# Attention weights turned over by products with a diagonal of reciprocals, in place of a scaling on VectorE and transposes

## The chip, the cores and the metric

The kernel runs on one core of one Trainium2 chip. The metric is the device time of one execution in microseconds. A core has TensorE for matrix products (the profile shows it as PE, and its weight loads as PEld), VectorE (DVE), ScalarE (ACT), GpSimd (POOL), and SyncE (SP), which issues the large transfers.

## The reference, cut to what matters

Two networks run one after the other on 256 tokens of width 1024. The change lies in the first of them (`first_block`, depth 2), and there only in its attention:

```
def attention(q, k, v, scale):
    ...
    def one_block(qi):
        s = jnp.einsum('bhgqd,bhkd->bhgqk', qi, k, preferred_element_type=jnp.float32) * scale
        p = jax.nn.softmax(s, axis=-1)
        return jnp.einsum('bhgqk,bhkd->bhgqd', p.astype(v.dtype), v)
```

There are 12 heads: 6 with a head width of 64 that share 2 key heads, and 6 with query and key width 96 and a value width of 64. In layer 0 both the 256 context tokens (which see 256 keys) and the 256 latent tokens (which see all 512 keys) go through attention. In layer 1 only the latent tokens do. Everything is computed in float32.

## The kernel before

One program with a list of instructions for each engine, written out by hand. The engines are tied together by semaphores alone, and each engine works through its list in order. The weights of the model stream through a ring of three 2 MB slots; ScalarE and VectorE split each granule of them into two parts, and most products on TensorE are three passes over such parts (lines 1367 to 1369).

The attention of layer `i` (lines 1548 to 1608 for TensorE) is a loop over steps `j`. A step has one pair of heads, one set of tokens and 128 queries, and so two units `u = 2j` and `2j+1`, one for each head. A unit has 128 queries in the partitions and its keys, 256 or 512, along the row. Layer 0 has 24 steps (12 with 256 keys, 12 with 512) and 48 units; layer 1 has 12 steps with 512 keys and 24 units. In its step `j` each engine does this:

- TensorE: the score products of units 2j and 2j+1 into banks 0 to 3 (line 1574; 64 rows for the first three pairs of heads, whose two products lie side by side in the array, 96 rows for the other three); in layer 0 now and then a part of a modulation row (lines 1326 and 1336); then, for units 2j-4 and 2j-3, once `p_ready` says that the unit's weights are ready, one 128x128 transpose for each 128 keys into bank 4 or 5 (line 1592); and every second step the product of the values with the transposed weights of the group before (line 1606, 256 columns).
- VectorE: the negated maximum of each row of units 2j and 2j+1 (line 2760); then, for units 2j-2 and 2j-1, the reciprocal of the row sum (line 2770) and the scaling of the whole row of weights by it (line 2771), which raises `p_ready`; then copies of finished outputs, modulation rows, and shares of the split of the coming weights.
- ScalarE: the copy of the transposed weights of units 2j-4 and 2j-3 out of their banks (line 2106); then the exponential of units 2j and 2j+1 with its row sum (line 2116).

The weights of a unit lie in one of four buffers (`weights(u)`: three in `pb`, one in `sq`). ScalarE writes unit `u` only after the transposes of unit `u-4` are done. `turns2` is a tile of 128x512 numbers that this stage does not use otherwise; its flat view `t2_flat` serves the stage before.

In all the two layers transpose 24 x 2 + 24 x 4 + 24 x 4 = 240 blocks of 128x128.

Of the kernel before, what the change touches and what calls it, by code (L numbers as in the profile page):

```python
# [11 lines left out]
ALU = mybir.AluOpType  # L12
# [3 lines left out]
P = 128  # L16
# [410 lines left out]
def program(nc, A, out):  # L427
# [5 lines left out]
    with ExitStack() as ctx:  # L433
# [53 lines left out]
        IDENT = cc("ident")  # L487
# [44 lines left out]
        t2_flat = turns2[:, :, :, :].rearrange("p a b c -> p (a b c)")  # L532
# [22 lines left out]
        qm_ss, qm_ms, qm_r, qm_r2, qm_c = (stat_of(o, MH) for o in (232, 256, 280, 304, 328))  # L555
        q_ms, q_r, q_r2 = (stat_of(o, GQ) for o in (352, 376, 400))
        sq_flat = sq[:, :, :].rearrange("p a t -> p (a t)")

        def squared_at(n, w):
            return sq_flat[:, 768 * (n % 2):768 * (n % 2) + w]  # L560
# [157 lines left out]
        p_ready = sem("p_ready")  # L718
# [43 lines left out]
        def weights(u):  # L762

            return pb[:, u % 4, :] if u % 4 < 3 else sq[:, 2, :]
# [57 lines left out]
        for _, _, product in granules:  # L822
            if product:
                b, n = use[product]
# [34 lines left out]
        for key in slots:  # L859
# [6 lines left out]
            else:  # L866
                b, n = use[last_product(key)]
# [383 lines left out]
        def _(pe):  # L1251
# [149 lines left out]
            for i in range(DEPTH):  # L1401
# [154 lines left out]
                for j in range(steps + 3):  # L1556
                    if j < steps:
                        pair, s = groups[j // 2]
                        if pair[0] == GQ and s == 0 and j % 2 == 0:

                            for h in range(MH):
                                await_drained(pe, (tag, "Tkm", h))
                                await_drained(pe, (tag, "Tqm", h))
                            for t in range(4):
                                await_drained(pe, (tag, "kvv", t))
                        q0, tiles = sets[s][0] + j % 2 * P, sets[s][1]
                        banks = [start_bank((tag, "s", 2 * j + e)) for e in range(2)]
                        for e, h in enumerate(pair):
                            if h < GQ:
                                rows = slice(HD * (h // 3), HD * (h // 3) + HD)  # L1570
                                lhs, rhs = qT[rows, h % 3, q0:q0 + P], kT[rows, 0:tiles * P]
                            else:
                                lhs, rhs = qmT[0:MQK, h - GQ, q0:q0 + P], kmT[0:MQK, h - GQ, 0:tiles * P]
                            fill(mm(banks[e][:, 0:tiles * P], lhs, rhs, start=True, stop=True), (tag, "s", 2 * j + e))  # L1574


                    if i == 0:
                        if j < 2:
                            mod_column(MOD_FIRST + j)
                        if j in MOD_STEPS:  # L1580
                            mod_products(MOD_STEPS[j], range(0, 4))
                        if j - 1 in MOD_STEPS:
                            mod_products(MOD_STEPS[j - 1], range(4, KC))
                        if j - 3 in MOD_STEPS:
                            mod_column(MOD_STEPS[j - 3])
                    if 0 <= j - 2 < steps:
                        tiles = sets[groups[(j - 2) // 2][1]][1]
                        for u in (2 * j - 4, 2 * j - 3):
                            b = start_bank((tag, "t", u))
                            pe.wait_ge(p_ready, p_base + u + 1)  # L1590
                            for t in range(tiles):
                                last = tr(b[:, t * P:(t + 1) * P], weights(u)[:, t * P:(t + 1) * P], IDENT)
                            fill(last, (tag, "t", u))
                    g, odd = divmod(j - 4, 2)
                    if 0 <= g < len(groups) and not odd:
                        pair, s = groups[g]
                        tiles = sets[s][1]
                        b = start_bank((tag, "o", g))
                        for u in range(4 * g, 4 * g + 4):
                            await_drained(pe, (tag, "t", u))  # L1600
                        for t in range(tiles):
                            for e, h in enumerate(pair):
                                rows = slice(64 * (h % 2), 64 * (h % 2) + 64)
                                v = v_tok[:, t, HD * (h // 3):HD * (h // 3) + HD] if h < GQ else \
                                    vm_tok[:, t, MV * (h - GQ):MV * (h - GQ) + MV]
                                last = mm(b[rows, 0:SEQ], v, weights_T(g, e)[:, t, :], start=(t == 0), stop=(t == tiles - 1))  # L1606
                        fill(last, (tag, "o", g))
                    c = j - steps
                    if 0 <= c < 2:
                        key = (tag, "pool", c)  # L1610
                        b = start_bank(key)
                        if c == 0:
                            pooled_seen[0] += 2 * (2 - s0)
                            pe.wait_ge(pooled, pooled_seen[0])
                        for s in range(s0, 2):
                            last = mm(b[:, s * SEQ:(s + 1) * SEQ], w_pool[:, i, c, :], upad[:, c, s, PAD:PAD + SEQ],
                                      start=True, stop=True)
                        fill(last, key)
# [756 lines left out]
        def _(dve):  # L2375
# [353 lines left out]
            for i in range(DEPTH):  # L2729
# [24 lines left out]
                for j in range(steps + 3):  # L2754
                    if j < steps:
                        keys = sets[groups[j // 2][1]][1] * P
                        for u in (2 * j, 2 * j + 1):
                            st = stat[:, 8 * (u % 8):8 * (u % 8) + 8]
                            await_bank(dve, (tag, "s", u))
                            V.tensor_reduce(st[:, 2:3], bank((tag, "s", u))[:, 0:keys], AX_X, ALU.max, negate=True)\  # L2760
                                .then_inc(nmax_ready, 1)
                    if i == 0 and j == 1:
                        for n in MOD_UNITS:
                            mod_biased(0, 4 * n, 4 * n + 4, ("modcol", n))
                    if 1 <= j <= steps:
                        keys = sets[groups[(j - 1) // 2][1]][1] * P
                        for u in (2 * j - 2, 2 * j - 1):
                            st = stat[:, 8 * (u % 8):8 * (u % 8) + 8]
                            await_drained(dve, (tag, "s", u))
                            link(V.reciprocal(st[:, 6:7], st[:, 4:5]))  # L2770
                            V.tensor_scalar(weights(u)[:, 0:keys], weights(u)[:, 0:keys], st[:, 6:7], None, ALU.mult)\
                                .then_inc(p_ready, 1)
                    if i == 0 and j - 1 in MOD_STEPS:
                        mod_row_copied(MOD_STEPS[j - 1])
                    if i == 0 and j - 3 in MOD_STEPS:
                        n = MOD_STEPS[j - 3]
                        mod_biased(0, 4 * n, 4 * n + 4, ("modcol", n))
                    c = j - steps - 1
                    if 0 <= c < 2:
                        key = (tag, "pool", c)  # L2780
                        await_bank(dve, key)
                        cols = slice(s0 * SEQ, TOK)
                        drain(V.tensor_scalar(mixT[:, 6 + c, cols], bank(key)[:, cols], gain(i, RA["ls"] + c), None,
                                              ALU.mult), key)
                    g, odd = divmod(j - 4, 2)
                    if 0 <= g < len(groups) and not odd:
                        pair, s = groups[g]
                        q0 = sets[s][0]
                        key = (tag, "o", g)
                        await_bank(dve, key)  # L2790
                        if pair[0] < GQ:
                            for h in pair:
                                rows = slice(64 * (h % 2), 64 * (h % 2) + 64)
                                last = V.tensor_copy(mixT[rows, h // 2, q0:q0 + SEQ], bank(key)[rows, 0:SEQ])
                        else:
                            last = V.tensor_copy(mixT[:, pair[0] // 2, q0:q0 + SEQ], bank(key)[:, 0:SEQ])
                        drain(last, key)
                    if j - 1 in MIX_STEPS[i]:
                        mix_rest()
                    if j == steps - 2:  # L2800
                        lo_to(first_gran["wout", i] + 1)
                    if j == steps + 1:
                        lo_to(first_gran["wout", i] + 2)
# [298 lines left out]
```

## Time and profile before

| | |
|---|---|
| time, median of 3 runs | 1700.58 us (1699.9 to 1702.26) |
| the profiled execution | 1699.19 us, with a span of 1697.4 us |
| PE busy | 1635.2 us (96%) |
| VectorE busy | 1149.6 us (68%) |
| ScalarE busy | 905.7 us (53%) |
| the two attention stages | about 129.4 to 211.1 us and 699.5 to 741.3 us |

Busy time of PE counts an instruction from its start to its modelled end, and ends overlap the next starts; so two back-to-back products take less from start to start than the duration that a row shows. A float32 product leaves two records of MATMUL in the trace, and a float32 transpose one.

### The profile page before, as it was taken

Reading aid. Unit: us, or ns where it says so; the run is one execution under the profiler, and the core shown is the slowest. Engines: PE = TensorE matmul, PEld = TensorE weight load, DVE = VectorE, ACT = ScalarE, POOL = GpSimd, SP = SyncE. Lnnn points to the kernel's source line nnn. Section 1 sums busy time; section 2 is a strip of 40 time slices with the busy share of each in tenths; the row PEclk is TensorE's granted clock in tenths of the full one; section 3 lists DMA queues with packets and bytes.
Section 4 is the critical chain, followed back from the end, with each engine's and each line's share of the span. In section 5 each row is a group of like instructions: output and inputs, shape, how many; then the busy total and the mean of one; then the engine's idle time right before and its main releaser. Section 6 shows DMA issues by size and latency. Waiting matters only on the chain.

```text
span 1697.4 us, 27974 instructions
## 1 busy us (share of the span) xinstructions
PE 1635.2 (96%) x10354; PEld 1403.1 (83%) x10354; DVE 1149.6 (68%) x2027; ACT 905.7 (53%) x1970; POOL 487.4 (29%) x936
## 2 busy tenths in 40 slices
PE   6998998999999999898999999999999999999998
PEld 3874586888888878577999887998899878999998
DVE  5668848877787347866555678785556787775555
ACT  4456725444353535756555666675444665764542
POOL 1432013000000022402000134277753161586720
PEclk9999999999999999999999999999999999999999
DMA  9524224555445222114545445442255445343450
GB/s 363 181 88 161 100 98 154 198 199 198 176 176 183 101 87 100 50 58 144 197 164 186 166 146 199 150 145 105 101 199 193 163 155 176 123 142 108 150 199 26
DMA packets 106393, 254.95 MB, mean 150 GB/s; under 512 B 2758, under 2 KB 9556, under 8 KB 103188
## 3 DMA queue, kind: packets, MB, share of 16 engines
q1 hardware_dynamic: 104890, 250.57, 41.4%
q0 software_dynamic: 1088, 2.56, 0.7%
q8 instruction: 84, 1.38, 0.3%
q14 instruction: 49, 0.40, 0.1%
q10 hardware_dynamic: 282, 0.04, 0.0%
HBM read 252.11 MB, written 1.05 MB: 149 GB/s over the span
## 4 chain that ended last, share of the span: by engine, by line
PE 51%; DVE 7%; ACT 3%; issue 1%; POOL 1%; DVEq 0%; ACTq 0%; POOLq 0%
PE ps L1367 12%; PE ps L1369 11%; PE ps L1368 11%; PE ps L1670 2%; PE ps L1671 2%; PE ps L1672 2%; DVE big_r L2522 2%; PE ps L1789 1%; PE ps L1792 1%; PE ps L1784 1%; ACT big_r L1901 1%; PE ps L1574 1%; DVE cst_r L2522 1%; DVE hT_r L2522 1%; PE ps L1606 1%
## 5 line engine op out<-in xcount | busy, mean ns | idle before, releaser
L1901 ACT ACTIVATE big_r<-ring 128x1024 fp32r<-128x1024 f32 (+2 forms) x224 | 234.9, 1049 | 373.1 <-PE ps L1369 352.9
L2522 DVE TENSOR_TENSOR big_r<-ring,big_r 128x1024 fp32r<-128x1024 f32 (+2 forms) x224 | 275.3, 1229 | 226.3 <-ACT big_r L1901 225.8
L1368 PE MATMUL ps<-big_r 128*128 128x256 f32 (+1 forms) x1064 | 352.9, 332 | 0.0
L1367 PE MATMUL ps<-hT_r,big_r 128*128 128x256 f32 (+1 forms) x768 | 245.7, 320 | 0.4 <-DVE big_r L2522 0.4
L1367 PE MATMUL ps<-big_r 128*128 128x256 f32 (+1 forms) x720 | 240.4, 334 | 3.6 <-DVE big_r L2522 1.7
L1369 PE MATMUL ps<-hT_r,big_r 128*128 128x256 f32 (+1 forms) x768 | 242.1, 315 | 0.0
L1369 PE MATMUL ps<-big_r 128*128 128x256 f32 (+1 forms) x720 | 237.9, 330 | 0.0
L1030 POOL TENSOR_TENSOR sq<-sq 128x256 f32<-128x256 f32 (+1 forms) x30 | 35.5, 1185 | 696.7 <-ACT sq L1858 695.1
L1368 PEld LDWEIGHTS ps<-big_r 128*128 128x128 f32 x1064 | 202.2, 190 | 18.3
L1367 PEld LDWEIGHTS ps<-hT_r,big_r 128*128 128x128 f32 x768 | 146.3, 190 | 9.6 <-issue 1.0
L1369 PEld LDWEIGHTS ps<-hT_r,big_r 128*128 128x128 f32 x768 | 146.2, 190 | 9.3
L1367 PEld LDWEIGHTS ps<-big_r 128*128 128x128 f32 x720 | 136.7, 190 | 18.5 <-issue 3.3
L1369 PEld LDWEIGHTS ps<-big_r 128*128 128x128 f32 x720 | 136.8, 190 | 12.8
L2522 DVE TENSOR_TENSOR cst_r<-ring,w_ukv_sb_r 128x1024 fp32r<-128x1024 f32 x70 | 88.5, 1265 | 54.1 <-ACT w_ukv_sb_r L1901 54.1
L1901 ACT ACTIVATE w_ukv_sb_r<-ring 128x1024 fp32r<-128x1024 f32 x70 | 74.0, 1057 | 85.5 <-PE ps L1369 73.4
L2488 DVE SCALAR_TENSOR_TENSOR pT<-ring,csilu,pT 128x512 f32<-128x512 f32 x168 | 118.4, 746 | 1.3
L1901 ACT ACTIVATE nt_r<-ring 128x1024 fp32r<-128x1024 f32 (+2 forms) x54 | 55.8, 1034 | 77.7 <-PE ps L1369 73.2
L2522 DVE TENSOR_TENSOR rstd_r<-ring,nt_r 128x1024 fp32r<-128x1024 f32 (+2 forms) x54 | 65.5, 1212 | 45.4 <-ACT nt_r L1901 45.3
L1367 PE MATMUL ps<-hT_r,w_ukv_sb_r 128*128 128x256 f32 x304 | 88.3, 290 | 0.0
L1369 PE MATMUL ps<-hT_r,cst_r 128*128 128x256 f32 x304 | 85.9, 283 | 0.0
L1368 PE MATMUL ps<-xT_r,nt_r 128*128 128x256 f32 x304 | 85.6, 282 | 0.0
L1368 PE MATMUL ps<-xT_r,w_ukv_sb_r 128*128 128x256 f32 x296 | 83.6, 283 | 0.0
(432 smaller groups left out, 4264.2 us busy)
## 6 DMA issues: line engine op xcount, KB each, us to landing
ring<-in_w_in SPq DMA_DIRECT2D x42, 2048.0 KB, 7.9
ring<-in_w_mlp SPq DMA_DIRECT2D x32, 2048.0 KB, 8.7
ring<-in_w_mod SPq DMA_DIRECT2D x24, 2048.0 KB, 7.9
ring<-in_w_out SPq DMA_DIRECT2D x4, 2048.0 KB, 7.9
ring<-in_w_out_a SPq DMA_DIRECT2D x4, 2048.0 KB, 7.9
ring<-in_w_out_b SPq DMA_DIRECT2D x4, 2048.0 KB, 8.1
ring<-in_w_o SPq DMA_DIRECT2D x4, 2048.0 KB, 8.1
ring<-in_w_in SPq DMA_DIRECT2D x2, 1536.0 KB, 14.2
```

Source lines behind the costliest of these rows:

```text
L1030: nc.gpsimd.tensor_tensor(sum_slot(0, T), sum_slot(0, T), sum_slot(k, T), ALU.add).then_inc(sq_summed, 1)
L1367: mm(b[:, 0:T], w_hi[:, k, :], hi(k), start=(j == 0), stop=False)
L1368: mm(b[:, 0:T], w_hi[:, k, :], lo(k), start=False, stop=False)
L1369: last = mm(b[:, 0:T], w_lo[:, k, :], hi(k), start=False, stop=(j == KC - 1))
L1574: fill(mm(banks[e][:, 0:tiles * P], lhs, rhs, start=True, stop=True), (tag, "s", 2 * j + e))
L1606: last = mm(b[rows, 0:SEQ], v, weights_T(g, e)[:, t, :], start=(t == 0), stop=(t == tiles - 1))
L1670: mm(o, x0, y_hi, start=(m == 0 and k == 0), stop=False)
L1671: mm(o, x0, y_lo, start=False, stop=False)
L1672: last = mm(o, x1, y_hi, start=False, stop=(m == 3 and k == 1))
L1901: act_fn(hi, raw, ACT.Copy).then_inc(hi_ready, 1)
L2488: ins = V.scalar_tensor_tensor(acc, w, c, acc, ALU.mult, ALU.add)
L2522: V.tensor_tensor(lo, raw, hi.bitcast(F32), ALU.subtract).then_inc(lo_ready, 1)
```

## The change

The row of weights is no longer scaled. VectorE instead scales the 128x128 identity by the reciprocals, which gives a matrix with the reciprocals on its diagonal (`normaliser(u)`, one of four in `turns2`), and raises `p_ready` after that. TensorE then computes the product of the transposed block of weights with this matrix, which is the transposed block with each query's column scaled. It writes the same bank, in the same place of the order. Nothing else in the order of any engine changes, and no wait is added or taken away.

```
+        def normaliser(u):
+
+            return t2_flat[:, P * (u % 4):P * (u % 4) + P]
...
                             b = start_bank((tag, "t", u))
                             pe.wait_ge(p_ready, p_base + u + 1)
                             for t in range(tiles):
-                                last = tr(b[:, t * P:(t + 1) * P], weights(u)[:, t * P:(t + 1) * P], IDENT)
+                                last = mm(b[:, t * P:(t + 1) * P], weights(u)[:, t * P:(t + 1) * P], normaliser(u),
+                                          start=True, stop=True)
                             fill(last, (tag, "t", u))
...
                             st = stat[:, 8 * (u % 8):8 * (u % 8) + 8]
                             await_drained(dve, (tag, "s", u))
                             link(V.reciprocal(st[:, 6:7], st[:, 4:5]))
-                            V.tensor_scalar(weights(u)[:, 0:keys], weights(u)[:, 0:keys], st[:, 6:7], None, ALU.mult)\
-                                .then_inc(p_ready, 1)
+                            V.tensor_scalar(normaliser(u), IDENT, st[:, 6:7], None, ALU.mult).then_inc(p_ready, 1)
```

## Rows read from the trace of the kernel before

**Rows 1.** The page, busy time: us, share of the span, instructions.

```profile
PE 1635.2 (96%) x10354; PEld 1403.1 (83%) x10354; DVE 1149.6 (68%) x2027; ACT 905.7 (53%) x1970; POOL 487.4 (29%) x936
```

**Rows 2.** Windows over both attention stages: length, busy us of each engine, clock.

```profile
core 0: us, PE busy (x) PEld busy (x) DVE busy (x) ACT busy (x) POOL busy (x), PEclk, DMA share, GB/s
129.40:143.00 13.60, 10.51 (x64) 4.75 (x64) 12.00 (x28) 6.73 (x21) 10.15 (x12) 1.00 0.72 281
143.00:203.00 60.00, 59.25 (x370) 32.45 (x368) 50.69 (x147) 40.75 (x120) 0.00 (x0) 1.00 0.30 106
203.00:211.10 8.10, 6.95 (x49) 4.89 (x49) 6.19 (x14) 6.41 (x14) 0.00 (x0) 1.00 0.01 2
699.50:706.80 7.30, 6.69 (x35) 3.39 (x36) 7.09 (x18) 6.30 (x17) 5.35 (x8) 1.00 0.00 0
706.80:732.80 26.00, 26.00 (x151) 15.04 (x149) 21.58 (x53) 18.55 (x46) 0.00 (x0) 1.00 0.01 2
732.80:741.30 8.50, 6.96 (x54) 4.69 (x53) 5.95 (x16) 6.76 (x16) 0.00 (x0) 1.00 0.01 3
```

**Rows 3.** The transposes' line, L1592: ns min/median/max, and who waits for them.

```profile
L1592 PEld LDWEIGHTS ps<-cst,pb x180: 137/140/144, 135.7 to 737.7; 128*128 128x128 f32 x180
L1592 PE MATMUL ps<-cst,pb x180: 270/273/331, 135.8 to 737.8; 128*128 128x128 f32 x180
...
L1592 PE MATMUL ps<-cst,sq x60: 271/273/300, 139.6 to 738.2; 128*128 128x128 f32 x60
...
  DVE pb L2771: 5.6, 7
```

**Rows 4.** Timeline of PE, second network: three float32 products of 128x128 blocks.

```profile
1107.59 0.39 PE L1765 MATMUL ps<-big,pT 128*128 128x128 f32 x2
1107.81 0.39 PE L1766 MATMUL ps<-big,pT 128*128 128x128 f32 x2
1108.04 0.39 PE L1767 MATMUL ps<-big,pT 128*128 128x128 f32 x2
```

**Rows 5.** L1765's weight loads: ns min/median/max.

```profile
L1765 PEld LDWEIGHTS ps<-big,pT x64: 188/191/192, 1087.8 to 1603.8; 128*128 128x128 f32 x64
```

**Rows 6.** Timeline of PE, end of layer 1's attention; idle before in brackets.

```profile
731.79 0.60 PE L1592 MATMUL ps<-cst,pb 128*128 128x128 f32 x4
732.23 0.60 PE L1592 MATMUL ps<-cst,sq 128*128 128x128 f32 x4
733.91 1.22 PE L1592 MATMUL ps<-cst,pb 128*128 128x128 f32 x8 [1.08 <-DVE pb L2771]
...
739.41 0.40 PE L1606 MATMUL ps<-rstd,big 128*64 128x256 f32 x1 [0.46 <-ACT nt L2106]
```

**Rows 7.** Timeline of PE, start of layer 0's attention.

```profile
135.77 0.41 PE L1592 MATMUL ps<-cst,pb 128*128 128x128 f32 x2 [0.76 <-DVE pb L2771]
136.56 0.41 PE L1592 MATMUL ps<-cst,pb 128*128 128x128 f32 x2 [0.39 <-DVE pb L2771]
...
141.97 1.22 PE L1592 MATMUL ps<-cst,pb 128*128 128x128 f32 x8 [0.76 <-DVE pb L2771]
```

**Rows 8.** Timeline of PE, the two other waits of layer 0.

```profile
164.63 1.22 PE L1592 MATMUL ps<-cst,pb 128*128 128x128 f32 x8 [0.60 <-DVE pb L2771]
...
204.13 1.22 PE L1592 MATMUL ps<-cst,pb 128*128 128x128 f32 x8 [1.25 <-DVE pb L2771]
```

**Rows 9.** Timeline of PE, layer 1: eight transposes at its start, and eight later.

```profile
700.64 1.40 PE L1592 MATMUL ps<-cst,pb 128*128 128x128 f32 x8
...
712.60 1.04 PE L1592 MATMUL ps<-cst,pb 128*128 128x128 f32 x8
```

**Rows 10.** Timeline of DVE: the scaling beside a busy POOL, and alone.

```profile
134.38 1.25 DVE L2771 TENSOR_SCALAR pb<-pb,stat 128x256 f32<-128x256 f32 x1
...
137.72 0.91 DVE L2771 TENSOR_SCALAR pb<-pb,stat 128x256 f32<-128x256 f32 x1
...
195.74 0.35 DVE L2771 TENSOR_SCALAR pb<-pb,stat 128x256 f32<-128x256 f32 x1
...
203.50 0.49 DVE L2771 TENSOR_SCALAR pb<-pb,stat 128x512 f32<-128x512 f32 x1
```

**Rows 11.** Waits in 129 to 212 us: total us, times, longest.

```profile
ACT pT L2106 <- PE ps L1592: 17.9, 11, 3.3
```

## The prediction, made before the run

> **What bounds the kernel now.** I read the busy shares first: PE is busy for 96% of the span and VectorE for 68% [rows 1], so the kernel as a whole is TensorE's. That share is an average, and the change touches two stages only, so I then cut the two attention stages into windows [rows 2]. Each has three parts. In the long middle parts (143 to 203 us and 706.8 to 732.8 us) PE is busy for 59.25 of 60.00 us and 26.00 of 26.00 us at a granted clock of 1.00, while VectorE has 50.69 and 21.58 us of work: TensorE sets the pace. At the starts it is the other way round: from 129.4 to 143 us PE has 10.51 of 13.6 us and VectorE 12.00, and from 699.5 to 706.8 us VectorE is at 7.09 of 7.30. At the ends neither is full. Next the question of who waits for whom at the changed lines. The transposes waited for the scaling 5.6 us in 7 waits [rows 3], and nearly all of that stands at the places shown in [rows 6 to 8]; ScalarE, which copies the transposed blocks out, waited for the transposes 17.9 us in layer 0 alone [rows 11]. So a slower turning-over is paid by TensorE directly through most of both stages, and a quicker preparation on VectorE pays only at the starts and in three other waits.
>
> **What one block costs before.** A row gives a transpose 273 ns [rows 3], but these overlap. Two groups of four start at 731.79 and 732.23 us [rows 6]: 0.44 us for four, 0.11 us for a block. Likewise eight take 1.04 us, and (1.04 - 0.27) / 7 is 0.11 [rows 9].
>
> **What one block costs after.** The trace has the very form elsewhere: a float32 product with 128x128 stationary weights and 128 moving columns [rows 4]. Each leaves two records, and the three start at 1107.59, 1107.81 and 1108.04 us: 0.45 us for two, 0.225 us for one; the rounding of the rows allows 0.22 to 0.23. I take 0.2225, twice the 0.11 us between its records (0.39 us for two less the 0.275 of one gives 0.11 to 0.12). So a block costs 0.1125 us more. 240 blocks [rows 3] make 27.0 us if TensorE is the bound at every one.
>
> A rule speaks to this. The Trainium skill, TensorE: Matmul & The Clock Gate, in Terms, says that the transpose mode is four times as fast for FP32 as the ordinary one. By that rule, with 0.2225 us for the product, a transpose would take 0.056 us and the change would cost 0.167 x 240 = 40 us. The row has 0.11 us for the transpose, so the row's factor of two goes into the sum.
>
> **Part by part.** Where TensorE waits for VectorE, the longer products fill the wait. I go through the stretches of [rows 2].
>
> - Middle parts: layer 0 has 16 of its 144 blocks before and 16 behind, layer 1 24 and 16 of its 96. That leaves 112 and 56: 168 x 0.1125 = +18.9 us. One wait of 0.60 us lies inside, at 164.63 us [rows 8]; the four products before it take 0.45 us longer and the diagonal is ready 0.2 us earlier (below), so it goes: -0.6. Together +18.3.
> - Start of layer 0: 16 blocks, +1.8 us of PE. But PE waits here five times for the scaling, 0.76, 0.39, 0.75, 0.39 and 0.76 us, the first two and the last in [rows 7]. VectorE sets the pace, beside a busy GpSimd (10.15 of 13.6 us). The second product of each pair starts after a wait, so most of the 1.8 us is hidden, and only some 0.9 us of it, at 142 us, comes after the last wait. VectorE itself gets quicker: four scalings of 256 columns that take up to 1.25 and 0.91 us here against 0.35 us alone [rows 10] become 128 columns wide. I take 0.35 to 0.4 us off each, 1.5 in all. Net -0.6 us.
> - Start of layer 1: 24 blocks, +2.7 us. Eight transposes take 1.40 us there against 1.04 later [rows 9], so 0.36 us in these eight is waiting, and the two steps behind them wait about as much; 1.2 us of waiting vanishes because TensorE becomes the slower. Net +1.5 us.
> - End of layer 0: 16 blocks, +1.8 us. The wait of 1.25 us at 204.13 [rows 8] shrinks by the 0.45 us of the four blocks before it and the 0.2 us of the quicker VectorE, and a short wait between the two units goes (0.13): net +1.0.
> - End of layer 1: 16 blocks, +1.8 us. The wait of 1.08 us at 733.91 [rows 6] has eight blocks before it, 0.9 us, and with 0.2 us from VectorE it is gone; the wait of 0.46 us for ScalarE's copy at 739.41 shrinks by some 0.3, and 0.1 goes between units. Net +0.3 to +0.4.
> - Restarts: a product's weight load takes 191 ns [rows 5], a transpose's 140 [rows 3]. In the row of products the load hides; at the head of a group, behind another shape, it shows. 36 steps x 0.05 us is 1.8 us; I keep +1.0, since the rest falls into waits.
>
> The sum is 18.3 - 0.6 + 1.5 + 1.0 + 0.3 + 1.0 = **+21.5 us**.
>
> **VectorE's own saving** is larger than what the path sees. A row of 512 takes 0.49 us and one of 256 0.35 us [rows 10], so 0.14 us for 256 columns; 128 columns would take 0.28. 48 units save 0.21 us and 24 save 0.07: 11.8 us. In the middle parts it is worth nothing, because VectorE already idles there (50.69 of 60 us). The identity is read in place of the weights, so ScalarE's buffers come free no later than before, except that TensorE holds them 0.45 us longer for a unit, and ScalarE, with 40.75 of 60 us, has room for that. No DMA is issued or moved.
>
> The profiled execution was 1699.19 us, 1.4 us under the median. From the median, 1700.6 + 21.5 = **1722.1**.
>
> **The rivals.**
> 1. *VectorE is the real bound.* Its lists hold the reductions, copies and splits that TensorE needs, and it is at 84% in the middle of layer 0. Then the doubled products hide, the 11.8 us come off, and the time is 1689. It speaks against this that PE's busy time leaves 0.75 us in 60, and that ScalarE waits 17.9 us for transposes. It decides only if PE has more than 0.45 us of hidden slack in a step of two key tiles and 0.9 us in one of four. 4%.
> 2. *The second record hides.* If a product cost what a transpose costs in this place, only the waits would change: 6.6 us of them at most, and about 2 us by what VectorE gives back; 1697 to 1701. The three rows in a line [rows 4] speak against it. 3%.
> 3. *More is absorbed.* Waits that the modelled ends hide (PE's 59.25 us of busy time count overlap) take up another 5 to 11 us: 1710 to 1716. 10%.
> 4. *The weight loads bind.* If a load must end before the next begins, a block costs 2 x 0.19 = 0.38 us, +0.27 a block and +65 us at most: 1765. In [rows 4] the records start every 0.11 us with those very loads, so 3%; the partial case, restarts dearer than I count and nothing absorbed (27.0 + 3.6), ends at 1731. Both together 6%.
> 5. *A transpose is quicker than its spacing.* If 0.11 us were set by the 140 ns of its weight load and half of it were slack of the array, the product would cost three blocks' time more, not one: 0.167 x 240 = 40 us, 1740. In the trace eight transposes and the products around them follow each other at 0.11 us whether they stand in fours or in eights [rows 6, 9], so I see no such slack: 2%. It is what the Trainium skill's factor of four (TensorE: Matmul & The Clock Gate, Terms) would give.
>
> **How the numbers follow.** The forecast, slower by 15 to 29 us, has 75%. Its low end has every wait at the changed lines absorbed (27.0 less 6.6 us of waits and 3.5 of waits hidden in modelled ends: 1717.5), its high end almost nothing absorbed and all restarts paid (27.0 + 1.8: 1729.4). The range 1715.5 to 1729.5 takes in the near edge of rival 3 and leaves out the rest of the rivals and the tails of the forecast, 2 in 10. A measurement of this kernel tells 0.2%, 3.4 us, from no change. Slower by more than that: 93%; within: 3%; faster: 4%.
>
> **What would show it.** In the profile after, the changed line should have 480 records in place of 240, 0.11 us apart, with weight loads of 190 ns. Attention of layer 0 should last about 12.5 us longer and that of layer 1 about 8.5; the stretches outside should keep their lengths. VectorE's busy time should fall by some 11 us with no gain from it, a diagonal should take 0.28 us, and the waits at 164, 204 and 734 us should shrink or go. Starts of units still 0.11 us a block, or attention stages that keep their lengths, would prove the sum wrong; a stage that grows by more than 27 us in total would show the loads or a wait that I do not see.

## The result, and the profile after

| | before | after |
|---|---|---|
| time, median | 1700.99 us (4 runs) | 1721.24 us (4 runs, 1720.43 to 1725.96) |
| ratio to before | | 1.0127, 95% interval 1.0113 to 1.0140 |
| the profiled execution: time | 1699.19 us | 1720.43 us |
| its span | 1697.4 us | 1718.6 us |

The kernel is slower by 20 to 22 us: the medians differ by 20.3 and the ratio makes 21.6. The forecast was 21.5.

The page of the kernel after, busy time (it answers to [rows 1]):

```profile
PE 1660.2 (97%) x10594; PEld 1432.9 (83%) x10594; DVE 1140.5 (66%) x2027; ACT 908.2 (53%) x1970; POOL 485.2 (28%) x936
```

PE has 240 records more and 25 us more of busy time; VectorE has 9.1 us less, and the kernel is no quicker for it.

Windows of the kernel after, cut where the stretches of [rows 2] ended (before and behind the middle of each stage):

```profile
core 0: us, PE busy (x) PEld busy (x) DVE busy (x) ACT busy (x) POOL busy (x), PEclk, DMA share, GB/s
127.60:141.70 14.10, 12.46 (x80) 7.04 (x80) 12.43 (x33) 6.93 (x21) 10.01 (x12) 1.00 0.71 274
141.70:212.60 70.90, 70.90 (x475) 45.78 (x474) 45.11 (x140) 42.39 (x118) 0.00 (x0) 1.00 0.25 90
212.60:222.80 10.20, 9.60 (x74) 7.49 (x72) 6.38 (x15) 7.10 (x14) 0.00 (x0) 1.00 0.01 2
707.80:720.30 12.50, 11.04 (x68) 7.25 (x68) 9.71 (x26) 8.45 (x21) 7.95 (x12) 1.00 0.00 1
720.30:750.60 30.30, 30.30 (x190) 20.15 (x189) 16.93 (x46) 18.45 (x44) 0.00 (x0) 1.00 0.01 1
750.60:761.60 11.00, 10.66 (x86) 8.47 (x84) 6.48 (x18) 7.17 (x16) 0.00 (x0) 1.00 0.00 1
```

The windows of layer 1 do not match one for one: [rows 2] begin at 699.5 us, but its first score product starts at 696.07 us, and the window from 707.80 us holds the whole start. TensorE now has no pause that the modelled ends leave visible in 70.9 us of layer 0 and 30.3 us of layer 1, at full clock. The time has gone into the two attention stages. The table gives their lengths from the first score product to the end of the last product with the values, read from the timeline of PE in each trace; "start" is the part up to the first product with the values.

| us | layer 0 | of it start | between the stages | layer 1 | of it start | behind |
|---|---|---|---|---|---|---|
| before | 81.7 | 13.7 | 484.9 | 45.3 | 10.9 | 956.0 |
| after | 95.2 | 14.1 | 484.9 | 53.8 | 12.6 | 957.0 |
| product alone | 96.0 | 14.5 | 485.5 | 56.1 | 14.6 | 956.9 |
| transposed twice | 94.8 | 14.4 | 486.5 | 55.5 | 14.4 | 955.7 |
| diagonal alone | 79.5 | 12.5 | 486.1 | 45.4 | 11.4 | 957.1 |
| no scaling | 76.6 | 10.2 | 486.3 | 44.5 | 10.8 | 957.2 |
| products twice | 124.7 | 16.0 | 486.4 | 75.1 | 17.9 | 957.2 |
| changed in layer 1 | 81.6 | 13.5 | 485.3 | 53.8 | 12.6 | 957.1 |

Layer 0 is 13.5 us longer and layer 1 is 8.5, 22.1 with unrounded lengths. The stretch between them has not changed. What is ahead of layer 0 took 1.8 us less in this execution and what is behind took 1.0 more, which leaves the 21.2 us by which the spans differ. Neither of these two comes from the change: in the other kernels of the table the stretch behind differs by as much, and layer 0 begins anywhere between 127.6 and 129.7 us.

One column, layer 1's start, needs care. The granted clock over layer 1's start was 1.00 before, after, with the products twice and with the change in layer 1, but 0.77 in the product alone, 0.76 transposed twice, 0.87 in the diagonal alone and 0.85 without scaling. Windows over that start, kernel before and product alone:

```profile
696.10:707.00 10.90, 8.85 (x44) 4.16 (x44) 9.59 (x22) 8.07 (x21) 8.44 (x12) 1.00 0.00 0
```

```profile
711.10:725.70 14.60, 14.02 (x68) 8.47 (x68) 11.11 (x25) 8.56 (x21) 8.59 (x12) 0.77 0.00 1
```

So this column, and layer 1's length with it, can be compared only between kernels of the same clock. In layer 0 all eight have 1.00.

The changed line, L1596 (it answers to [rows 3]; ns min/median/max, then what TensorE waited for before it, us and times):

```profile
L1596 PEld LDWEIGHTS ps<-turns,pb x360: 186/192/192, 133.8 to 757.6; 128*128 128x128 f32 x180
L1596 PE MATMUL ps<-turns,pb x360: 272/275/377, 133.9 to 757.7; 128*128 128x128 f32 x180
...
L1596 PE MATMUL ps<-turns,sq x120: 275/275/347, 137.6 to 758.6; 128*128 128x128 f32 x120
...
  DVE turns L2776: 2.0, 4
```

The last row is a wait of TensorE for the diagonal, and so is the last row of [rows 3] one for the scaling. There are 480 records where there were 240. Timeline of PE, two groups of the kernel after:

```profile
183.90 1.95 PE L1596 MATMUL ps<-turns,pb 128*128 128x128 f32 x16
...
214.24 2.02 PE L1596 MATMUL ps<-turns,pb 128*128 128x128 f32 x16 [0.60 <-DVE turns L2776]
```

Sixteen records, eight blocks, take 1.95 us: (1.95 - 0.275) / 15 is 0.112 us a record and 0.223 us a block. The second row is the place of the wait of 1.25 us in [rows 8]; it is 0.60 us now.

### The profile page after: what moved, and what is told of

It reads as the page before. It is cut to its first block, busy times and chain, and to the rows that moved or that the text cites. A ratio compares the mean times of both kernels' runs of the same rounds, so it can differ in the third digit from the quotient of the medians.

```text
span 1718.6 us, 28454 instructions
## 1 busy us (share of the span) xinstructions
PE 1660.2 (97%) x10594; PEld 1432.9 (83%) x10594; DVE 1140.5 (66%) x2027; ACT 908.2 (53%) x1970; POOL 485.2 (28%) x936
## 4 chain that ended last, share of the span: by engine, by line
PE 51%; DVE 6%; ACT 3%; issue 1%; POOL 1%; DVEq 0%; ACTq 0%; POOLq 0%
PE ps L1371 11%; PE ps L1373 11%; PE ps L1372 11%; PE ps L1675 2%; PE ps L1677 2%; PE ps L1676 2%; DVE big_r L2527 2%; PE ps L1596 1%; PE ps L1794 1%; PE ps L1797 1%; PE ps L1789 1%; PE ps L1578 1%; ACT big_r L1906 1%; DVE cst_r L2527 1%; DVE hT_r L2527 1%
## 5 line engine op out<-in xcount | busy, mean ns | idle before, releaser
L1372 PEld LDWEIGHTS ps<-big_r 128*128 128x128 f32 x1064 | 202.2, 190 | 18.3
```

The source lines that it names most:

```text
L1372: mm(b[:, 0:T], w_hi[:, k, :], lo(k), start=False, stop=False)
```

## The experiments

All times are set against runs of the kernel before on the same chip, with ratios of medians and 95% intervals.

**TensorE's half alone.**

```
-   last = tr(b[:, t * P:(t + 1) * P], weights(u)[:, t * P:(t + 1) * P], IDENT)
+   last = mm(b[:, t * P:(t + 1) * P], weights(u)[:, t * P:(t + 1) * P], IDENT,
+             start=True, stop=True)
```

> TensorE's half of the change alone: the blocks are turned over by float32 products, but with the plain identity, and VectorE still scales the whole row of weights. Theory (TensorE's occupancy is the cost, 0.11 us more for each of 240 blocks, and VectorE's shorter work is worth 1 to 2 us in all): 1722 to 1724, 1 to 2 us above the changed kernel. Rival (VectorE's relief carried much of the result, so the product is dearer than 0.22 us): 1727 or more. In the trace the product's records should start 0.11 us apart, and the waits for the scaling should be longer than in the changed kernel by about 0.2 us each.

Measured: 1725.4 us, ratio 1.0144 (1.0127 to 1.0161), which is +24.5 us. That is over the range of the theory by 1.4 us and below the rival's. TensorE's half alone costs more than both halves together, by 2.9 us as the ratios have it. The traces do not show that VectorE's relief is worth that much: against the changed kernel layer 0 is 0.7 us longer and layer 1 behind its start 0.2 us, both at a clock of 1.00, which is 0.9 us, and the other 2.1 us stand in layer 1's start, where the clock was 0.77 against 1.00. TensorE waited for the scaling 2.7 us in 5 waits, against 2.0 in 4.

**VectorE's half alone.**

```
-   V.tensor_scalar(weights(u)[:, 0:keys], weights(u)[:, 0:keys], st[:, 6:7], None, ALU.mult)\
-       .then_inc(p_ready, 1)
+   V.tensor_scalar(normaliser(u), IDENT, st[:, 6:7], None, ALU.mult).then_inc(p_ready, 1)
```

> VectorE's half alone: it scales the identity into the diagonal matrix and signals, but TensorE transposes the unscaled weights with the plain identity. This leaves the normalisation of the softmax out of the result. Theory (in the middle of both stages TensorE sets the pace, so the narrower instruction is worth about 0.2 us at each wait for it and nothing elsewhere): 1698 to 1700, 1 to 3 us below the kernel before. Rival (VectorE is the bound and its 9 to 12 us of saved time count): 1689 to 1692.

Measured: 1697.4 us, ratio 0.9984 (0.9974 to 0.9993), which is -2.7 us. The rival, in which VectorE's saved work would all count, is out. The trace has layer 0 shorter by 2.2 us, 1.2 of them at the start (the part on the prediction shows why this does not carry over to the changed kernel).

**Every transpose twice.**

```
    last = tr(b[:, t * P:(t + 1) * P], weights(u)[:, t * P:(t + 1) * P], IDENT)
+   last = tr(b[:, t * P:(t + 1) * P], weights(u)[:, t * P:(t + 1) * P], IDENT)
```

> The kernel before with every transpose issued twice into the same place, so that a block occupies TensorE for 0.22 us as the product does, with the transpose's own weight load of 140 ns and VectorE as before. Theory (only the occupancy counts): the same time as the product with the identity beside the row scaling, 1722 to 1724. Rival (the product's longer weight load of 190 ns shows at each restart, 36 steps and more): 2 to 3 us less than that kernel, 1720 to 1721.

Measured: 1722.3 us, ratio 1.0125 (1.0110 to 1.0140), which is +21.3 us. That lies in the theory's range, and at the same time 3.1 us under the product alone, which is the rival's difference. The intervals of the two kernels overlap, but the two stages in the traces differ by 1.2 and 0.6 us, with like clocks (0.77 and 0.76 at layer 1's start). The changed line of both, product alone first:

```profile
L1592 PEld LDWEIGHTS ps<-cst,pb x360: 186/192/333, 135.8 to 763.1; 128*128 128x128 f32 x180
```

```profile
L1592 PEld LDWEIGHTS ps<-cst,pb x180: 137/140/226, 135.7 to 762.1; 128*128 128x128 f32 x180
```

The weight loads are the 192 and 140 ns that were expected. The occupancy of 0.11 us more for each block makes the bulk, whatever instruction brings it. The small rest of 1.8 us is not the load alone. Sixteen records of the doubled transposes start 0.109 us apart (185.51 to 187.15 us), those of products 0.112, which makes some 1.1 us in 480 records. The remaining 0.7 us stand at the heads of groups: of the 34, about half take 0.05 us more beyond the spacing, and the others nothing.

**Every product twice.**

```
    last = mm(b[:, t * P:(t + 1) * P], weights(u)[:, t * P:(t + 1) * P], normaliser(u),
              start=True, stop=True)
+   last = mm(b[:, t * P:(t + 1) * P], weights(u)[:, t * P:(t + 1) * P], normaliser(u),
+             start=True, stop=True)
```

> The changed kernel with every turning product issued twice into the same place. Theory (TensorE's occupancy is paid one for one, 0.2225 us for each of 240 products, once the waits are gone): 1721.2 + 53.4 less at most 3 us of waits that are left, 1771 to 1775. Rival (the stage still has slack that absorbs work): 1765 or less.

Measured: 1774.8 us, ratio 1.0428 (1.0412 to 1.0444), 53.6 us above the changed kernel's 1721.2. The runs of the kernel before beside them differ too, 1701.9 and 1701.0 us; by the ratios the difference is 51.2 us, and the two stages grew by 50.7. In layer 0's start 1.9 us of 3.6 are paid, so waits still hid 1.7. Everywhere else 224 products cost 48.8 us, 0.218 us each, where 0.2225 would make 49.8. In this trace they start 0.224 us apart (201.62 to 204.08 us, twelve of them). So TensorE's time is paid in full but for the waits that the changed kernel had left. What is left of the wait for VectorE in this kernel:

```profile
  DVE turns L2778: 0.7, 1
```

**No scaling on VectorE.**

```
-   link(V.reciprocal(st[:, 6:7], st[:, 4:5]))
-   V.tensor_scalar(weights(u)[:, 0:keys], weights(u)[:, 0:keys], st[:, 6:7], None, ALU.mult)\
-       .then_inc(p_ready, 1)
+   V.reciprocal(st[:, 6:7], st[:, 4:5]).then_inc(p_ready, 1)
```

> The kernel before with the scaling on VectorE left out: only the reciprocal is taken, and it signals; TensorE transposes the unscaled weights. This leaves the normalisation out of the result. It shows the most that any relief of VectorE at this place can bring. Theory (VectorE's work is on the path at the starts of the stages, beside a busy GpSimd, and before three more waits): 1693 to 1697, up to 4 us below the kernel with the diagonal alone, nearly all of it before the first output product of each layer. Rival (VectorE's work counts throughout, 35 us of it gone): below 1690.

Measured: 1693.8 us, ratio 0.9949 (0.9932 to 0.9965), 7 to 9 us below the kernel before. Some 35 us of work (the sum of the L2771 groups) is gone from VectorE and a fourth of it comes off the time. Against the diagonal alone layer 0 is 2.9 us shorter, 2.3 of them at its start. Timeline of PE at that start, without any scaling:

```profile
134.97 0.66 PE L1592 MATMUL ps<-cst,pb 128*128 128x128 f32 x4
...
136.61 0.44 PE L1592 MATMUL ps<-cst,pb 128*128 128x128 f32 x2
136.88 0.38 PE L1592 MATMUL ps<-cst,sq 128*128 128x128 f32 x2
...
138.70 1.04 PE L1592 MATMUL ps<-cst,pb 128*128 128x128 f32 x8
```

None of these has a pause ahead of it; in [rows 7] each had one, and the last group came at 141.97 us.

**The change in layer 1 alone.**

```
-   last = mm(b[:, t * P:(t + 1) * P], weights(u)[:, t * P:(t + 1) * P], normaliser(u), ...)
+   if i:
+       last = mm(b[:, t * P:(t + 1) * P], weights(u)[:, t * P:(t + 1) * P], normaliser(u), ...)
+   else:
+       last = tr(b[:, t * P:(t + 1) * P], weights(u)[:, t * P:(t + 1) * P], IDENT)
```

VectorE's line has the same `if i`: the diagonal in layer 1, the row of weights in layer 0.

> The change in layer 1 alone; layer 0 scales the rows and transposes as before. Theory (the two stages add up independently): 8 to 9.5 us above the kernel before, 1709 to 1710, with layer 0's stage of the old length and the stage of layer 1 about 8.5 us longer. Rival (the shift of layer 0 carried something into the stages between): 1712 or more, or 1706 or less.

Measured: 1709.3 us, ratio 1.0043 (1.0028 to 1.0058), which is +7.4 us on an interval of 4.8 to 9.9. The trace has the layers at 81.6 and 53.8 us, the length before and the length after. The stages add up independently; the +7.4 us lies a little under the theory's 8, within its interval.

**Products of rounded operands.** The exponentials and the diagonal are written and read in the rounded float32 form, which rounds the attention weights and the reciprocals.

```
+   pb_r, sq_r = rounded_view("pb", [P, 3, 512]), rounded_view("sq", [P, SQ, 512])
+   turns2_r = rounded_view("turns2", [P, 4 * 2 * HD])
...
-   last = mm(b[:, t * P:(t + 1) * P], weights(u)[:, t * P:(t + 1) * P], normaliser(u), ...)
+   last = mm(b[:, t * P:(t + 1) * P], weights_r(u)[:, t * P:(t + 1) * P], normaliser_r(u), ...)
```

> The changed kernel with both operands of the turning products, the exponentials and the diagonal, written and read in the rounded float32 form that the kernel's large products use. This rounds the attention weights and the reciprocals to that form. Theory (the cost of the change is the second record and the two columns' time of a full float32 product): one record for each block, 0.11 us or less apart, so the time falls back to that of the kernel before less VectorE's saving, 1697 to 1700. Rival (the weight load of 190 ns binds when a product has only 128 columns): 0.19 us for a block, 13 to 19 us more than the kernel before, 1713 to 1720.

Measured: a median of 1705.4 us, ratio 1.0023 (1.0001 to 1.0045), with single times from 1696.2 to 1713.5. The changed line in the trace of this kernel:

```profile
L1606 PEld LDWEIGHTS ps<-turns_r,pb_r x180: 186/192/338, 133.8 to 740.3; 128*128 128x128 f32 x180
L1606 PE MATMUL ps<-turns_r,pb_r x180: 271/276/630, 133.8 to 740.3; 128*128 128x128 f32 x180
```

One record for a block. Eight of them, at 193.17 us, were followed 1.03 us later by the next product (0.13 us a block with the change of shape):

```profile
193.17 1.11 PE L1606 MATMUL ps<-turns_r,pb_r 128*128 128x128 f32 x8
194.20 1.08 PE L1621 MATMUL ps<-pT,big 128*64 128x256 f32 x8
```

In the kernel before, eight transposes at 192.01 us were followed 1.02 us later. So the second record is what the full product adds, and the load of 192 ns does not bind at 128 columns. But neither theory had the spread. Windows of the same trace:

```profile
core 0: us, PE busy (x) PEld busy (x) DVE busy (x) ACT busy (x) POOL busy (x), PEclk, DMA share, GB/s
127.60:139.40 11.80, 9.79 (x59) 4.61 (x60) 10.25 (x26) 6.22 (x20) 10.10 (x12) 1.00 0.79 307
139.40:149.60 10.20, 10.20 (x41) 6.18 (x42) 5.85 (x22) 5.60 (x18) 0.00 (x0) 0.51 0.04 17
```

The granted clock is 0.51, the lower of its two levels of 1.2 and 2.4 GHz, for 10.2 us of layer 0's attention, which took 84.3 us. It was 1.00 there in the kernel before, in the kernel after and in every other trace of this document. In the ten runs the time follows the mean clock of each: 1696.2 us at 0.992, 1701.2 at 0.989, 1705.0 at 0.986, 1709.1 at 0.983, 1713.5 at 0.980. The 19 runs of the kernel before beside them have clocks of 0.989 to 0.994.

**Three more kernels on that clock.** First, rounded products in layer 1 only (the same `if i` as above).

> Layer 0 as in the kernel before; layer 1 with the diagonal and products of operands in the rounded float32 form. Theory (the spread of the kernel with rounded products in both layers came from TensorE's clock falling to half in layer 0's attention, whose start has the most pauses, and one record of 0.11 us costs what a transpose does): within 2 us of the kernel before, 1699 to 1702, with a spread like its own. Rival (rounded products lower the granted clock wherever they stand): a median above 1703 and single times above 1706.

Measured: 1701.8 us, ratio 1.0005 (0.9991 to 1.0018), single times 1698.2 to 1706.9 at clocks of 0.993 to 0.986. The median is the theory's, the single times are the rival's. Where the clock was low in the slower runs is not known, since they have only a mean over the whole run. Second, rounded products in both layers with something for TensorE to do while it waits:

```
+   if u < 8:
+       for _ in range(4):
+           tr(b[:, 0:P], IDENT, IDENT)
    pe.wait_ge(p_ready, p_base + u + 1)
```

> Rounded products in both layers as before, and ahead of each wait for the first eight units of a layer TensorE transposes the identity four times into the bank that the unit then overwrites (0.44 us a unit, where it waited for VectorE). Theory (the pauses at the starts let the granted clock fall, as the trace of the kernel with rounded products showed from 139.4 to 149.6 us): the spread goes, every granted clock is 0.99 or more, and the time is 1696 to 1700, for the filler fits mostly into waits. Rival (the rounded products themselves lower the clock, wherever the pauses are): single times above 1705 with clocks below 0.988 again.

Measured: 1701.9 us, ratio 1.0008 (0.9999 to 1.0017), 1700.1 to 1705.3, clocks 0.989 to 0.992. The low clocks are gone in eleven runs, but the median is 2 us over the theory's range. The profiled run shows why the theory is half right; windows of it:

```profile
129.30:142.00 12.70, 12.64 (x88) 7.61 (x88) 11.05 (x30) 6.96 (x21) 10.04 (x12) 1.00 0.75 293
691.80:705.50 13.70, 12.12 (x41) 6.70 (x39) 7.79 (x17) 6.69 (x19) 10.74 (x15) 0.50 0.00 1
```

In layer 0 the pauses are filled (12.64 us busy of 12.70) and the clock stays at 1.00. At the head of layer 1 it was low for 13.7 us all the same, and layer 1's start took 15.4 us there against 11.1 without filler. How much of this is the filler and how much the clock is not shown. Third, full products for the first eight units of each layer and rounded ones behind:

```
+   if u < 8:
+       last = mm(..., weights(u)[:, t * P:(t + 1) * P], normaliser(u), start=True, stop=True)
+   else:
+       last = mm(..., weights_r(u)[:, t * P:(t + 1) * P], normaliser_r(u), start=True, stop=True)
```

> The diagonal everywhere; full float32 products for the first eight units of each layer, products of rounded operands for the rest. Theory (only the starts are in danger, and a full product keeps the clock up there): 1700 to 1704, with a spread like that of the kernel before and clocks of 0.99 or more; 56 blocks at 0.11 us more, less VectorE's relief. Rival (the rounded products themselves lower the clock): single times above 1708 with clocks below 0.988.

Measured: 1704.1 us, ratio 1.0017 (1.0008 to 1.0026), 1701.5 to 1706.3, clocks 0.989 to 0.993, as the theory had it within 0.1 us and 0.001. In its trace the clock is 1.00 through layer 0, so rounded products in the long middle part did not lower it. At layer 1's start it is low here too, with full products:

```profile
695.50:710.20 14.70, 14.11 (x70) 8.55 (x71) 10.13 (x26) 8.55 (x21) 8.18 (x12) 0.77 0.00 1
```

So the low clock at the head of layer 1 is not a matter of rounding: it also stands in the product alone (0.77), in the doubled transposes (0.76) and in the diagonal alone (0.87), which have no rounded product. The low stretch in layer 0 was seen only with rounded products at the start and no filler, in one trace. That these products and the pauses bring it about together fits all the kernels here, but is argued and not shown. No version with the normalisation in it beats the kernel before.

## Why the prediction was right, point by point

**TensorE sets the pace in the middle of both stages.** Right, and shown twice over: 240 products more lengthen the two stages by 50.7 us, 48.8 of them outside layer 0's start, and a doubled transpose costs nearly what a product does. The forecast had +18.3 us for the middle parts. Between the first product with the values and the group at 202.27 us (212.59 after) layer 0 grew by 11.7 us, for 108 blocks; the working gives 108 x 0.1125 - 0.6, 11.6. Behind its start, layer 1 grew by 6.9 us in all, where the working has 6.3 for its 56 blocks and 0.3 to 0.4 for its end. In all layer 0 grew by 13.5 us where about 12.5 were expected, and layer 1 by the 8.5 that were.

**0.2225 us for a product, 0.11 for a transpose.** Right: 0.223 in the row at 183.90 and 0.224 between the doubled products. The other network's products showed the price before they were in this place, with 275 ns and loads of 191 (192 now). The Trainium skill's factor of four (TensorE: Matmul & The Clock Gate, Terms) does not hold here: by rows it is 2.0. The estimate of 40 us that the prediction worked out from that factor is far above the 20 to 22 us measured.

**The start of layer 0.** Wrong by about 1 us: -0.6 was forecast, +0.5 measured. The hiding was right. In the product alone the groups behind the first, third and last waits start 6.30, 9.32 and 12.51 us into the stage, against 6.32, 9.33 and 12.52 before: nothing of the longer products is paid up to the last wait, and 0.8 us behind it, where 0.9 were forecast. The step that failed is VectorE's part, "0.35 to 0.4 us off each, 1.5 in all". In the changed kernel the same three groups start at 6.24, 9.20 and 12.19 us, so it gave back 0.3 us. The four scalings took 1.25, 0.69, 0.91 and 0.69 us before, and the four diagonals 1.18, 0.69, 0.86 and 0.70: 0.1 us less in all. Timeline of VectorE and of GpSimd, kernel after:

```profile
132.53 1.18 DVE L2776 TENSOR_SCALAR turns<-cst,stat 128x128 f32<-128x128 f32 x1
...
135.81 0.86 DVE L2776 TENSOR_SCALAR turns<-cst,stat 128x128 f32<-128x128 f32 x1
```

```profile
132.36 1.27 POOL L1155 TENSOR_TENSOR big<-big 128x512 f32<-128x512 f32 x1
133.71 2.88 POOL L1161 TENSOR_TENSOR big<-big,cst 64x256 f32<-64x256 f32 x4
```

Beside GpSimd the diagonal is hardly shorter than the row of 256 in [rows 10]. The diagonal alone gained 1.2 us at this start, but its third diagonal met GpSimd at another moment:

```profile
137.48 0.29 DVE L2775 TENSOR_SCALAR turns<-cst,stat 128x128 f32<-128x128 f32 x1
```

With 0.29 us there, in place of 0.86, the next diagonal came sooner too. So the 1.2 us are no measure of what VectorE gives back in the changed kernel.

**VectorE's saving.** 11 to 12 us were forecast. The rows of the changed line add up to 34.6 us before and 23.8 after, 10.8 less; the engine's busy time, which counts the overlap of neighbouring rows once, fell by 9.1. Why the two differ by 1.7 us is not shown. The saving was said to be worth nothing in the middle parts, and the diagonal alone, with -2.7 us in all, agrees: the two waits of [rows 8] shrank from 0.60 and 1.25 us to 0.40 and 1.06, the 0.2 us each that the working has.

**The start and end of layer 1, and the waits.** +1.5 us were forecast for the start, 1.6 measured, both at a clock of 1.00; the wait at 734 us went (there is none in front of the products there), the one at 204 us fell by 0.65 us to 0.60 as worked out, and the one for ScalarE's copy by 0.12 us to 0.34 where 0.3 was forecast. Layer 0's end cost +1.4 us for +1.0.

**Restarts.** +1.0 us forecast. Of the 1.8 us between the product alone and the doubled transposes, some 0.7 us stand at heads of groups and the rest in the spacing of the records, for which the working had no term. How much of it the changed kernel pays was not measured by itself. The 3.5 us of waits hidden in modelled ends, in the low end of the range, are shown by no run, and the 6.6 us of waits for the scaling there are 6.2 in the trace.

The errors, 1 us too low at layer 0's start and some tenths too low at its end, put the stages 22.1 us longer, where the parts without the restarts make 20.5; the restart term of 1.0 covers most of that gap, but not for the reason it was given. That the total came out at 20 to 22 us, so near to 21.5, is in part luck: the executions differ by 1 to 2 us outside the stages, and 3.4 us is what a measurement tells apart. Of the rivals, the absorbed one (10 to 16 us) is ruled out by the doubled products, VectorE as the bound by the diagonal alone, and the hidden second record by the rows. Weight loads that bind are ruled out by records 0.112 us apart, and the quicker transpose by the total.

## What to carry to other kernels

A float32 product that stands in for a float32 transpose doubles TensorE's time for the block, so it only pays where TensorE waits; price it from a row of the same form elsewhere in the trace, by starts and not by durations. Read the pace of the very stage: work taken from an engine that idles there gave back a fourth at most, at the starts and at a few single waits. Before a difference of 1 to 3 us between two traces is given to a cause, compare the granted clock of the stage in both. Before rounding a product to make it cheaper, look at the granted clock of the stage it stands in, since the saving can be lost to it.

## What the runs showed of the hardware that was not expected

- A VectorE scaling that begins during a GpSimd instruction on SBUF can last until that instruction ends, at 128 columns as at 256: the 1.18 us row of 128 columns ends at 133.71 us and GpSimd's at 133.63, and the 1.25 us row of 256 before at 135.63 us and GpSimd's at 135.47. Alone they take 0.29 and 0.35 us.
- In the one trace with rounded products at the start of layer 0's attention and no filler, the granted clock was 0.51 for 10.2 us; with full products or transposes there it was 1.00. A run's mean clock of 0.980 in place of 0.992 went with 17 us more.
- The clock over layer 1's start was between 0.70 and 0.87 in eight of the twelve traces, with transposes, full products and rounded ones alike, and 1.00 in four.
- A weight load of 192 ns does not keep records of 128 columns apart: full products start every 0.112 us.
